# A two-layer hybrid transformer step: attention queries one head further ahead, the vector engine's branch moved before the last expert octet, and the filter loads of layer two moved forward

## The reference, cut to what matters

```python
def trunk_layer(x, cond, rope, ctx_cache, p):
    ...
    h = x * (1 + sc1) + sh1
    mixed, ckv, kpe = token_mixers(h, rope, ctx_cache, p)      # gMLP, long convolution, attention
    x = layer_norm(ALPHA * x + g1 * mixed, p['ln1_g'], p['ln1_b'])
    h = x * (1 + sc2) + sh2
    x = layer_norm(ALPHA * x + g2 * hier_moe(h, p), p['ln2_g'], p['ln2_b'])

def one_block(qs):                                             # attention, 8 heads
    s = jnp.einsum('bqhd,bkhd->bhqk', qn_b, k_nope) + jnp.einsum('bqhr,bkr->bhqk', qp_b, k_pe)
    prob = jax.nn.softmax(s.astype(F32) * scale, axis=-1).astype(v.dtype)
    return jnp.einsum('bhqk,bkhd->bqhd', prob, v)

def hyena_filter_spectrum(L, p):                               # the filter of the long convolution
    ...
    filt = (hid @ p['hy_f_w3'].astype(F32)).reshape(L, HY_ORDER, 2, HY_WIDTH)
    filt = filt * jnp.exp(-t * deltas)[:, None, None, :]
```

## Time and profile before

| | us |
|---|---|
| median of three runs | 1266.63 (1262.53 to 1271.31) |
| the profiled execution, its own time | 1264.24 |
| its span in the trace | 1262.4 |
| PE busy in the span | 1032.8 |
| DVE busy | 538.1 |
| ACT busy | 351.2 |
| POOL busy | 86.9 |

### The profile page before, as it was taken

One profiled execution on the slowest core, in us unless ns is written; L12 is line 12 of the kernel. 1 busy time (PEld: TensorE's weight loads), 2 busy tenths in 40 slices (PEclk: granted clock), 3 DMA queues, 4 the chain that ended last, 5 costly groups with the idle time before them and its releaser, 6 DMA issues.

```text
span 1262.4 us, 19787 instructions
## 1 busy us (share of the span) xinstructions
PE 1032.8 (82%) x8178; PEld 609.3 (48%) x8178; DVE 538.1 (43%) x1218; ACT 351.2 (28%) x731; POOL 86.9 (7%) x97
## 2 busy tenths in 40 slices
PE   4788887887977999999973997687977999999970
PEld 3356566655444634444331757454445634444320
DVE  5540133376564233332648106456564224242446
ACT  3120001245131343323331203145132332333331
POOL 0110000010140000000001500000140000000000
PEclk9989889899987989999995998888987979999995
DMA  9856669540356879999946314010356879898941
GB/s 350 325 211 270 266 255 337 210 178 18 133 202 247 334 288 419 369 421 380 421 194 251 119 36 137 1 50 17 133 209 252 323 279 406 349 421 358 420 167 50
DMA packets 48619, 309.52 MB, mean 245 GB/s; under 512 B 6427, under 2 KB 6684, under 8 KB 15748
## 3 DMA queue, kind: packets, MB, share of 16 engines
q1 hardware_dynamic: 39516, 274.08, 54.5%
q0 software_dynamic: 7856, 31.85, 7.3%
q10 hardware_dynamic: 1144, 2.19, 0.5%
HBM read 303.11 MB, written 4.98 MB: 244 GB/s over the span
## 4 chain that ended last, share of the span: by engine, by line
PE 65%; DVE 13%; DMA 13%; ACT 4%; issue 3%; ACTq 0%; POOL 0%; SPq 0%; DVEq 0%; POOLq 0%
PE bank L936 18%; PE bank L915 8%; PE bank L831 7%; PE bank L689 5%; PE bank L1024 4%; PE bank L675 3%; DMA ring<-in_moe_gate_up 3%; DMA arena<-in_b_mod 3%; DMA ring<-in_w_in 3%; PE bank L700 2%; PE bank L765 2%; PE bank L774 2%; PE bank L599 2%; PE bank L927 1%; PE bank L616 1%
## 5 line engine op out<-in xcount | busy, mean ns | idle before, releaser
L915 PE MATMUL bank<-sel,h_hi 128*128 128x384 f32 x192 | 84.2, 439 | 9.4 <-DVE sel L1881 9.4
L616 PE MATMUL bank<-ring,arena 128*32 128x64 f32 x3072 | 62.0, 246 | 29.4 <-DMA ring<-in_w_mod 19.9
L831 PE MATMUL bank<-ring,act_t 128*128 128x512 f32 x192 | 84.1, 594 | 0.0
L915 PE MATMUL bank<-sel,h_lo 128*128 128x384 f32 x192 | 79.1, 412 | 0.0
L915 PEld LDWEIGHTS bank<-sel,h_hi 128*128 128x128 f32 x192 | 64.5, 336 | 29.5 <-issue 23.3
L616 PEld LDWEIGHTS bank<-ring,arena 128*32 128x32 f32 x3072 | 55.2, 127 | 43.1 <-issue 20.7
L1341 ACT ACTIVATE arena<-bank 128x384 f32<-128x384 f32 x64 | 31.4, 491 | 160.1 <-PE bank L915 160.1
L936 PE MATMUL bank<-ring,arena 128*32 128x512 f32 x480 | 61.1, 628 | 16.5 <-DVE act_t L1919 11.3
L689 PE MATMUL bank<-act_t,ring 128*128 128x384 f32 x192 | 66.7, 510 | 3.1 <-DMA ring<-in_w_in 3.1
L1024 PE MATMUL bank<-y_hi,selT 128*128 128x512 f32 x144 | 61.6, 428 | 7.0 <-DVE y_lo L1942 6.7
L915 PEld LDWEIGHTS bank<-sel,h_lo 128*128 128x128 f32 x192 | 65.3, 340 | 0.0
(11 more groups left out here) (309 smaller groups left out, 1769.3 us busy)
## 6 DMA issues: line engine op xcount, KB each, us to landing
ring<-in_moe_gate_up SPq DMA_DIRECT2D x60, 1024.0 KB, 8.9
ring<-in_w_mod SPq DMA_DIRECT2D x48, 1024.0 KB, 9.2
region_k<-in_moe_gate_up SPq DMA_DIRECT2D x44, 1024.0 KB, 8.4
ring<-in_moe_down SPq DMA_DIRECT2D x32, 1024.0 KB, 9.4
arena<-in_moe_down SPq DMA_DIRECT2D x28, 1024.0 KB, 8.9
arena<-in_moe_gate_up SPq DMA_DIRECT2D x20, 1024.0 KB, 10.2
ring<-in_w_in SPq DMA_DIRECT2D x10, 1024.0 KB, 7.7
ring<-in_w_out SPq DMA_DIRECT2D x8, 1024.0 KB, 5.3
```

What stands on the lines that cost most here:

```text
L616: mm = pe.matmul(ps[MOD_BANK[g]][32 * j:32 * j + 32, c * 64:c * 64 + 64], cT[:, k, :], w[:, k, j * 64:j * 64 + 64], start=(k == 0), stop=( ...
L831: mm = pe.matmul(ps[2 * t + half][:, :], act_t[:, 2 * c + k, t * P:(t + 1) * P], w[:, k, half * 512:(half + 1) * 512], start=(c == 0 and k ...
L915: mm = pe.matmul(ps[gather_bank(o, k)][:, 0:TOK], src[:, t, k:D:K8], sel[:, t, :, :].rearrange("p v n -> p (v n)"), start=(t == 0 and i == ...
```

## The change

There are three edits.

First, attention. `query(3)` moves ahead of the loop, and in turn hh the engines ask for `query(hh + 4)` after the transposes of head hh (TensorE) or after their copies (ScalarE). On VectorE the division becomes a function `normalized`; a turn is now maxima of hh + 2, division of hh + 1, query of hh + 4.

Second, VectorE's branch on `units` moves ahead of its last octet, which is written twice, once in each arm. The other engines branch where they did; TensorE waits once more at the end of the general path.

Third, `w3` and `decay` of layer two are issued by GpSimd once chunk 47 of the 48 (`TAPS_AFTER = 47`) is through both `done` and `over`, `dft` gets a semaphore of its own (`dft_in`, awaited by `filter_spectra`, L599), and `decay` moves to the `arena`, in a part of weight slot 1.

```diff
+TAPS_AFTER = 1 + max(c for c in range(len(CHUNKS)) if slot_of(c) < 2)
...
-    decay = region_v[:, 0:768].rearrange("p (t n) -> p t n", t=TT)
+    decay = arena[:, A_MLA:A_MLA + TT * CH].rearrange("p (t n) -> p t n", t=TT)
...
             if l == 0:
                 pool.wait_ge(s["chunk_done"], 3)
-                load_taps()
+            else:
+                pool.wait_ge(e["done"], len(CHUNKS) * (l - 1) + TAPS_AFTER)
+                pool.wait_ge(e["over"], len(CHUNKS) * (l - 1) + TAPS_AFTER)
+            pool.dma_start(w3, a["hy_f_w3"][l]).then_inc(s["taps_in"], 16)
+            pool.dma_start(decay, a["decay"]).then_inc(s["taps_in"], 16)
...
         def filter_taps(l):
-            pe.wait_ge(s["taps_in"], 48 * (l + 1))
+            pe.wait_ge(s["taps_in"], 32 * (l + 1))
             pe.wait_ge(s["hid"], at("hid", l))
+            if l > 0:
+                pe.wait_ge(e["acc"], SUMS * OCTS * l)
...
         def filter_spectra(l):
             pe.wait_ge(s["filt_eo"], at("filt_eo", l))
+            pe.wait_ge(s["dft_in"], 16 * (l + 1))
...
+            query(3)
             for hh in range(HEADS):
-                if hh + 3 < HEADS:
-                    query(hh + 3)
                 if hh + 2 < HEADS:
                     scores(hh + 2)
                 probs_turned(hh)
+                if hh + 4 < HEADS:
+                    query(hh + 4)
...
-            for hh in range(HEADS):
+            def normalized(hh):
                 c, pr = SOFT_COLS[hh % 2], probs[hh % 2]
                 dve.wait_ge(s["pexp"], at("pexp", l, hh + 1))
...
+            normalized(0)
+            query(3)
+            for hh in range(HEADS):
                 if hh + 2 < HEADS:
                     maxima(hh + 2)
-                if hh + 3 < HEADS:
-                    query(hh + 3)
+                if hh + 1 < HEADS:
+                    normalized(hh + 1)
+                if hh + 4 < HEADS:
+                    query(hh + 4)
...
-            dve.wait_ge(e["acc"], SUMS * OCTS * (l + 1))
+            for o in range(1, OCTS - 1):
+                oct_work(o)
             dve.wait_ge(s["regs"], at("regs", l))
             units = dve.value_load(xi[0:1, 0:1], min_val=0, max_val=2 * TOK)
             with dve.If(units >= P + 1):
+                oct_work(OCTS - 1)
+                last_oct_work()
+                dve.wait_ge(e["acc"], SUMS * OCTS * (l + 1))
                 r = rest[l]
...
+            with dve.Else():
+                steps[0] = linked
+                oct_work(OCTS - 1)
+                last_oct_work()
+            dve.wait_ge(e["acc"], SUMS * OCTS * (l + 1))
```

More of the change, by code:

```diff
@@ L323, in build @@
     s = {name: sem(name) for name in PER}
-    for name in ("x_in", "cond_in", "mlp_in", "taps_in", "cT", "mod_zero", "bmod_in", "mod_sum", "mod_out", "mod0_out",
+    for name in ("x_in", "cond_in", "mlp_in", "taps_in", "dft_in", "cT", "mod_zero", "bmod_in", "mod_sum", "mod_out", "mod0_out",
                  "ln_var", "ln_std", "ln_scale", "normed", "pool_step", "x0", "chunk_done", "small_in", "cache_in",
@@ L477, in _ @@
                 pool.wait_ge(s["v_raw"], at("v_raw", l - 1))
-            def load_taps():
-                pool.dma_start(w3, a["hy_f_w3"][l]).then_inc(s["taps_in"], 16)
-                pool.dma_start(decay, a["decay"]).then_inc(s["taps_in"], 16)
-                pool.dma_start(dft, a["dft"]).then_inc(s["taps_in"], 16)
             if l == 0:
                 pool.wait_ge(s["chunk_done"], 3)
-                load_taps()
+            else:
[3 more added lines that the diff above has]
+            pool.dma_start(decay, a["decay"]).then_inc(s["taps_in"], 16)
+            if l == 0:
+                pool.dma_start(dft, a["dft"]).then_inc(s["dft_in"], 16)
                 pool.wait_ge(s["mod0_out"], 16 * MOD_OUTS)
@@ L1170, in _ @@
                     rest_scatter(1, 17)
+                pe.wait_ge(r["summed"], REST_SUMMED * ROUNDS * OCTS)
     @block.scalar
@@ L1560, in filter_taps @@
         def filter_taps(l):
-            dve.wait_ge(s["taps_in"], 48 * (l + 1))
+            dve.wait_ge(s["taps_in"], 32 * (l + 1))
             for t in range(TT):
@@ L1982, in _, with oct_work @@
             copy(7)
-            for o in range(1, OCTS):
+            def oct_work(o):
                 c = CHUNK_AT["G", o, 0]
@@ L2036, in _, with last_oct_work @@
                 copy(c + 11)
-            last_oct, c = OCTS - 1, len(CHUNKS) - 4
-            gate(last_oct)
-            copy(c)
-            choice(last_oct, 0)
-            copy(c + 1)
-            choice(last_oct, 1)
-            for i in range(3):
-                y_rest(last_oct, i)
-            copy(c + 2)
-            summed(last_oct, 0)
-            copy(c + 3)
-            for i in range(3, BLOCKS):
-                y_rest(last_oct, i)
-            summed(last_oct, 1)
-            dve.wait_ge(e["acc"], SUMS * OCTS * (l + 1))
+            def last_oct_work():
+                last_oct, c = OCTS - 1, len(CHUNKS) - 4
+                gate(last_oct)
+                copy(c)
+                choice(last_oct, 0)
+                copy(c + 1)
+                choice(last_oct, 1)
+                for i in range(3):
+                    y_rest(last_oct, i)
+                copy(c + 2)
+                summed(last_oct, 0)
+                copy(c + 3)
+                for i in range(3, BLOCKS):
+                    y_rest(last_oct, i)
+                summed(last_oct, 1)
+            for o in range(1, OCTS - 1):
+                oct_work(o)
             dve.wait_ge(s["regs"], at("regs", l))
             units = dve.value_load(xi[0:1, 0:1], min_val=0, max_val=2 * TOK)
+            linked = steps[0]
             with dve.If(units >= P + 1):
+                oct_work(OCTS - 1)
+                last_oct_work()
+                dve.wait_ge(e["acc"], SUMS * OCTS * (l + 1))
                 r = rest[l]
@@ L2059, in _ @@
                     mul, shaped = REST_MUL * turn, REST_SHAPED * turn
-                    picked = [experts_of(o, UNITS * (step + b)) for b in range(2)]
+                    late_picked = [experts_of(o, UNITS * (step + b)) for b in range(2)]
                     def rest_copy(i):
```

2 lines of the change are left out of this document (1 added, 1 removed).

## The result

The changed kernel takes 1226.93 us, the median of 4 runs (1223.69 to 1230.1), beside 1264.58 for 4 runs of the kernel before: ratio 0.971, 95% interval 0.968 to 0.975, so 36 us less (32 to 41). Measured again in another series it was 1232.63 beside 1263.87: ratio 0.977 (0.975 to 0.980), 29 us less (25 to 32). Predicted were 30.1 us and 1236.

A forecast was written before the change was run, and what follows sets the result against it. Waits where the chain leaves TensorE were taken as what the edits can remove: 7 + 10 (attention) + 10 (border) + 3.1 (end) = 30.1 us off 1264.2 gives 1234.1; the median lies 2.4 above, so 1236, range 1226 to 1250.

The forecast's parts named there:

- the sum: Whole kernel: attention 7 + 10, border 10, end 3.1, together 30.1 us gained.
- The ring: Attention loop: VectorE's query waits behind maxima, maxima for scores, scores behind TensorE's query; 5.9 us a turn, cut by the edit.
- The hand-followed turns: Attention, scores of heads 2 to 7 in the new order, followed operation by operation: 22 us in all.
- one dip costs about 1 us, and I take one in each layer: Attention: allowance for a lower TensorE clock, taking gains of 7.8 and 11.2 us to 7 and 10.
- 0.6 for the clock: Border: projection may start at 1.2 GHz after TensorE idles; 0.6 us taken off 10.6, giving 10.
- 5.4 of them from the branch: Border: moving VectorE's branch gives 5.4 us of the projection's 10.6 us earlier start.
- The theory for the branch alone, 9.4 us: Forecast for the early-branch run: 5.9 us less between the layers, dft issued earlier too, and 3.5 at the end.
- 0.5 us left predicted: After VectorE's last sum: unconditional branch to the next instruction and wait for e_acc still cost 0.5 us.
- the fourth rival's margin: Border: TensorE's own branch delays taps harmlessly until 669.9, 11.5 us after its last matmul; counted within the range.
- the rival on the other side: Third octet's gate: slow fetch amid the weight stream, hidden up to 13.8 us, slower than before from 29 us; chance 0.02.
- A fetch at the arm's end: VectorE's arm end: unconditional branch fetches again, 6.9 us less gain, 1243 us; chance 0.10.
- a ring over ScalarE: Attention: query waits for ScalarE's copies, now behind the transposes; gain 7 instead of 17 us, 1246 us; chance 0.12.

The follow-up runs named there:

- vector order: Kernel before with VectorE's swap alone (query ahead of maxima), TensorE and ScalarE keeping their order: 1247.1 us, ratio 0.984.
- joined wait: Changed kernel with TensorE's taps of layer two waiting for dft as well, w3 and decay still early: 1240.61 us, ratio 0.981 to the kernel before.
- filter alone: Kernel before with the third edit whole (early w3 and decay loads, dft's own semaphore, decay in the arena): 1253.67 us, ratio 0.989.
- its two pieces tried alone: Kernel before with decay in the arena only: 1265.69 us, ratio 1.001; with dft on its own semaphore only: 1259.08 us, ratio 0.998.

## Why the prediction was right

By stages the change gives 34.5 us, where the sum had 30.1 and its upper bound 34.8. The first median, 1226.93, lies only 0.9 us inside the range; the profiled execution of that series had a front 6.0 us shorter than the kernel before, which no term of the sum covers. The second series, 1232.63, lies nearer the forecast.

**Attention: 17 predicted, 20.1 measured.** The ring was the right reading: cutting it alone (vector order) gives 17.4. The hand-followed turns, 4.7, 4.0, 5.7, 3.6 and 4.0 us, came out in the changed trace as 4.4, 3.9, 5.6, 3.7 and 4.0. The term that was off is "one dip costs about 1 us, and I take one in each layer": in the seven executions with the edit the stage is longer than 50.0 once in fourteen, and that one dip cost 1.6 us, at a granted clock of 0.97 (joined wait, layer two). The bounds, 5 to 8.8 and 6 to 12, held 8.3 and 11.8. What layer two gained over layer one is the clock: with the old ring it took 61.8 us at a granted clock of 0.92 and 58.4 at 0.97 (filter alone), with the new order 50.0 at 1.00. A second ring, over ScalarE's copies, exists too, but with VectorE's swap alone; the rival had such a ring in the changed kernel, whose turns show none.

**Border: 10 predicted, 10.9 measured.** VectorE finishes h 665.84 - 645.14 = 20.7 us after its last sum, where it took 685.95 - 659.35 = 26.6: 5.9 us, all of the branch's idle time, 5.4 predicted. The projection follows h by 672.60 - 665.84 = 6.8 us, where it took 11.7: 5.0 us, the filter loads. Predicted were 6.6 us and 0.6 for the clock. What ends last there is not quite what the prediction had: VectorE's tile 1 is done at 672.43, and the projection is released by ScalarE's copies of the transposes, 0.1 us later. The low clock fell on the transposes (0.55 from 665.9 to 672.6) and not on the projection (1.00 from 672.6 to 676.0).

But "5.4 of them from the branch" is no price that the branch has by itself. Alone it gives nothing there (38.5 against 37.9 to 39.6 without it), the filter loads alone give 7.4, and the two together 10.9; on top of the filter loads the branch gave 3.5 (31.0 - 27.5), as it had cost only 3.62 us in that execution. The theory for the branch alone, 9.4 us, took the 8.32 us of dft for a time that moves with its issue; it was the end of a busy stream of transfers, so an earlier issue only made it longer (14.2). With the taps off that stream, h is late next, as the prediction had it, and h does move with the branch. So the sum held because both edits were made.

**The branch: 0.5 us left predicted, 0.04 measured.** The unconditional branch to the next instruction is not seen at all, so the end gains 3.5 and not 3.1. The row from which the 0.5 set out has 0.13 us of "issue" but no record of a branch, and no run shows a cost of that kind. The branch is passed while the sums still run: in layer two VectorE's next wait (L2146) is recorded at 1190.44, and the last sum starts at 1190.63. TensorE's own decision is 3.80 us of idle time before the taps, 5.93 were taken; it stays off the path, as the fourth rival's margin said. The fetch ahead of the last octet is hidden (16.4 us until ScalarE releases the gate of the third), so the rival on the other side never came near.

**The rivals.** A fetch at the arm's end, a ring over ScalarE, a slow fetch in the stream and late taps: the changed trace shows none of them. What the prediction didn't have is the spread of the front, 261.5 to 270.9 us over 14 executions, which is as large as a whole term of the sum; with the spread of the experts' stretches it is of the size by which the two series differ (36 and 29 us). Whether the filter edit has a part in it stays open: the seven executions with the whole of it lie at 261.5 to 268.5 (mean 265.0), the seven others at 265.5 to 270.9 (mean 268.1), while neither of its two pieces tried alone brought the first query below 267. The spread doesn't arise where the edit works in layer one: when the taps are made and TensorE begins the spectra (L599 of the kernel before), the fourteen executions stand at 68.1 to 69.1 us. It opens behind that, up to some 220 us, where the chain of the kernel before has six waits of 4.9 to 9.3 us for loads of w_in and w_mod.

## What to carry to other kernels

A DMA's time from issue to landing is no property of that DMA: look at what else is in the stream, and ask whether an earlier issue lands earlier or only waits longer. Two edits at one place are worth what they give together; undo each alone before giving either a price. An engine's decision is best put where it waits for another anyway, and an order on an in-order engine is checked by writing down which ring each instruction closes, on every engine that it passes.

## What the runs showed of the hardware that was not expected

The branch has no fixed price. A far jump left VectorE idle for 5.7 to 6.7 us where the DMA share over that time was 0.84 to 0.92 (six executions), for 3.6 and 4.5 us at 0.45 and 0.50, and for 3.5 to 3.7 us at the end of layer two, where it was 0.03 or less (eight executions); a near one 1.0 to 1.4. That the transfers are what makes it longer is likely and not shown by a run of its own.

VectorE's operations on 128x256 with both inputs in SBUF, 0.42 us each, took 1.94 and 2.57 us while GpSimd's 128x1024 multiplication and addition (L463 and L464, 2.34 and 2.42 us) ran (the rows at 672.63 to 675.18 above); L1576 just ahead of them, which reads a bank, took its usual 0.47 us. They lie behind the start of the projection here, so they cost nothing there.
